# Memory keys before their norm, and a second cross product in the mixer's last row

## The chip, the core and the metric

The kernel runs on one NeuronCore of a Trainium2 chip. The metric is the device time of one execution in microseconds (us). TensorE (PE in the profile) multiplies, VectorE (DVE) and ScalarE (ACT) work element by element, GpSimd (POOL) splits weights, and SyncE (SP) issues nearly all transfers. Each engine runs its own instructions in order; engines meet through semaphores only.

## The reference

One layer on `x` (2048 tokens, width 1024), with a memory of 256 tokens:

```
h = x + W_out [ HGRN2 heads (4) || sliding-window attention heads (8) ](RMSNorm(x, g1))
h = h + CrossAttention_4heads(RMSNorm(h, g2), RMSNorm(mem, gm))
h = h + W_down relu(W_up RMSNorm(h, g3))^2
```

For the cross attention, `kv = RMSNorm(mem, gm) @ wkv`; the first 512 columns are the keys of four heads, each normed again over its 128 entries and scaled by `k_norm_g`; the other 512 are the values. RMSNorm divides a token's vector by the root of its mean square and multiplies by a gain for each of the 1024 entries.

## The kernel before

Matrices lie transposed, 128 rows to a partition tile, tokens along the free dimension. A product of the layer is made from two parts of each operand, a high part rounded to a shorter format and the low rest: for each 128-column panel of weights TensorE runs hi x hi and hi x lo, interleaved, and then lo x hi, 24 matmuls of 512 tokens in all. In an order, `m5.0`, `m5.1`, `m5.2` are the two halves of the first sixteen and the last eight.

There are four functions in a row, each with a block for each engine: `prepare` (norms and projects the memory, norms the first block of the input, makes the rope tables), `mixer` (four blocks of 512 tokens, 22 panels each, with the recurrent and window attention woven in), `cross` and `mlp`. Since an engine never waits at their borders but for semaphores, the border is only a place in each engine's own list.

**`prepare`.** SyncE issues all loads at once: `memT`, the constants, the gains `vec`, half of the key weights `wk`, the input block `hT`, the other half, the values' weights `wv`, the mixer's first two panels. ScalarE squares the memory's eight tiles, VectorE adds them, TensorE sums over partitions with a matrix of ones (L664), ScalarE and VectorE make the root (ScalarE gives a guess from Ln and Exp, VectorE one Newton step), and VectorE multiplies memory, gain `gm` and root into `mn` (L612). Then TensorE makes the keys of heads 0 to 2 (16 passes each), the total of the input's squares (L675), the keys of head 3, the values of the first 128 tokens, the totals of the squared keys, and the other values. ScalarE copies each head's keys out of its bank and squares them. For the input, ScalarE squares (L541) and VectorE adds (L619); behind the total come four ScalarE steps and two of VectorE, and then for each of the eight tiles VectorE's application (L642), ScalarE's high part `hi` and VectorE's low part `lo`. ScalarE's list goes on with the high part of the first mixer panel (`whi`, L560), the first values, the keys' root, the rope tables, the other values. VectorE ends with the keys' root and `memk` (L657). SyncE stores the rope tables, `memk` and `memv` to HBM, and only then goes on to the mixer's panels.

**`mixer`.** The order of each engine's steps is written out by hand in `ORDERS`, one string for each engine and block. `m` makes a product in one of two banks, `t` takes it out, `w` splits a panel's high part on ScalarE (GpSimd makes the low part), `u` turns a tile of probabilities (TensorE transposes, ScalarE copies), `p` multiplies by the values, `T`, `D`, `S`, `o` are the recurrent heads' steps, `A` takes the attention out. ScalarE's list ahead of the first block begins "w18 w19 t17 ...", and TensorE's begins with m17 to m21 of the first block. Three steps of the last row belong to the next stage: `X` and `Y` make the high part of the cross stage's panels 0 and 1 on ScalarE, `X` on GpSimd the low part of panel 0, and `M` on TensorE the first cross product.

At the end of the mixer, ScalarE's step `A3` takes out the last attention tile and issues its store and that of the last recurrent tile. SyncE waits for all four stores of the last row, in

```
            turn(NBLK - 1, True, False)
            for s in stored:
                sp.wait_ge(s.sem, s.at(NBLK - 1, 0))
```

and then begins the list of `cross`: it loads `memk` and `memv`, and then panel 3 as soon as both parts of panel 1 are made. Panel 2 is loaded already. Cross product n (m1, m2, ...) uses panel n in its first turn, in bank n % 2.

Of the kernel before, what the change touches and what calls it, by code (L numbers as in the profile page):

```python
# [22 lines left out]
ALU = mybir.AluOpType  # L23
# [3 lines left out]
P = 128  # L27
# [44 lines left out]
def panel_at(role, u):  # L72
# [96 lines left out]
        "X",  # L169
    ),  # L170
}

# [208 lines left out]
def layer(nc, xT, memT, pos, con_d, vec_d, sinks_d, w_mix, w_cross, w_mk, w_mv, w_mlp, outT):  # L381
# [7 lines left out]
    with ExitStack() as ctx:  # L389
        def sb(name, shape, dt=F32):  # L390
# [10 lines left out]
                  cross_hi=ctx.enter_context(nc.semaphore("c_panel_hi_ready")),  # L401
                  mlp_hi=ctx.enter_context(nc.semaphore("m_weight_hi_ready")),
# [32 lines left out]
def prepare(nc, block, sems, sh, memT, pos, con_d, vec_d, sinks_d, w_mk, w_mv, rope_d, mem_d, xT, w_mix):  # L435
# [9 lines left out]
    with ExitStack() as ctx:  # L445
# [17 lines left out]
        rv = sb("p_rv", [P, 5, MEM])  # L463
        rr = sb("p_rr", [P, 5, MEM])
        ru = sb("p_ru", [P, 5, MEM])
        ksq = sb("ksq", [P, HEADS, MEM])
        kraw = sb("kraw", [P, HEADS, MEM])
        key_mean, key_guess, key_root = (t[:, 1:1 + HEADS, :].rearrange("p h t -> p (h t)") for t in (rv, rr, ru))
# [29 lines left out]
        sh["first_ready"] = s_xhi, s_xln, s_act  # L498

        @block.sync  # L500
        def _(sp):
# [11 lines left out]
            sp.wait_ge(s_kn, 1)  # L513
# [6 lines left out]
        def _(act):  # L520
# [10 lines left out]
            act.activation(rv[:, 0, :], bank[0][:, 0:MEM], ACT.Identity, scale=1.0 / D_MODEL, bias=eps[:])  # L531
            act.activation(rr[:, 0, :], bank[0][:, 0:MEM], ACT.Ln, scale=1.0 / D_MODEL, bias=eps[:]).then_inc(s_act, 1)
            act.wait_ge(s_act, 1)
            act.activation(rr[:, 0, :], rr[:, 0, :], ACT.Exp, scale=-0.5).then_inc(s_r0, 1)
# [18 lines left out]
            act.wait_ge(s_mk, HEADS)  # L553
            act.activation(kraw[:, HEADS - 1, :], bank[HEADS][:, 0:MEM], ACT.Copy)
            act.activation(ksq[:, HEADS - 1, :], bank[HEADS][:, 0:MEM], ACT.Square).then_inc(s_kc, 1)
# [6 lines left out]
            act.activation(memv[:, 0, :], bank[5][:, :], ACT.Copy).then_inc(s_vc, 1)  # L562
            for n in range(HEADS // 2):
                act.wait_ge(s_tot, 3 + n)
                act.activation(key_mean[:, n * TB:(n + 1) * TB], bank[1 + n][:], ACT.Identity, scale=1.0 / P, bias=eps[:])
                act.activation(key_guess[:, n * TB:(n + 1) * TB], bank[1 + n][:], ACT.Ln, scale=1.0 / P, bias=eps[:]).then_inc(s_act, 1)
# [8 lines left out]
            act.activation(memv[:, 1, :], bank[6][:, :], ACT.Copy).then_inc(s_vc, 1)  # L575

        @block.vector
        def _(dve):
# [8 lines left out]
            chained(dve.memset(eps[:], EPS))  # L587
            for k in range(1, KT):
# [5 lines left out]
            dve.wait_ge(s_con, 32)  # L594
# [13 lines left out]
            chained(dve.scalar_tensor_tensor(ru[:, 0, :], rr[:, 0, :], -0.5, rr[:, 0, :], ALU.mult, ALU.mult))  # L608
            chained(dve.tensor_tensor(ru[:, 0, :], ru[:, 0, :], rv[:, 0, :], ALU.mult))
            chained(dve.scalar_tensor_tensor(ru[:, 0, :], ru[:, 0, :], 1.5, rr[:, 0, :], ALU.add, ALU.mult))  # L610
# [79 lines left out]
def mixer(nc, block, sems, sh, xT, w_mix, rope_d, y_d, w_cross, lows_d):  # L690
# [17 lines left out]
    with ExitStack() as ctx:  # L708
# [767 lines left out]
        def _(pe):  # L1476
# [43 lines left out]
            def cross_make(blk, part):  # L1520
# [6 lines left out]
                for k in range(KT) if part == 2 else range(part * KT // 2, (part + 1) * KT // 2):  # L1527
# [3 lines left out]
                    if part < 2:  # L1531
                        pe.matmul(PROJ[0][:], w[:, 0, cols], lo[:, k, :], start=False, stop=False)
# [1779 lines left out]
```

## Time and profile before

| | |
|---|---|
| runs | 2503.6, 2501.66, 2501.6 us; median 2501.66 us |
| the profiled execution | 2495.6 us, its span 2493.8 us |
| granted clock of TensorE, mean | 0.998 of 2.4 GHz |
| `prepare` on TensorE | 11.07 to 47.05 us |
| the mixer on TensorE | 47.05 to 816.4 us |

The span goes from the first to the last instruction of the profiled execution; times in the rows are counted from its start.

### The profile page before, as it was taken

The numbers are of one execution on the slowest core, as the hardware profiler recorded it, in microseconds if no ns is written. First come the engines' busy times: TensorE is split into PE (matmuls) and PEld (weight loads), VectorE is DVE, ScalarE is ACT, GpSimd is POOL, SyncE is SP. The second block draws the span as 40 slices with busy tenths as digits, with TensorE's granted clock in tenths as the row PEclk, the third lists the DMA queues.
The fourth block names the chain that finished last, engine by engine and source line by source line (L and its number), as shares of the span: only waits on it lengthen the run. The fifth ranks groups of instructions, "written<-read, shape, count | busy, mean of one in ns | idle before, by whom it ended". The sixth has DMA issues, their size and how long they took to land.

```text
span 2493.8 us, 39390 instructions
## 1 busy us (share of the span) xinstructions
PE 2454.1 (98%) x14110; PEld 2014.8 (81%) x14110; DVE 1735.3 (70%) x3014; ACT 1136.4 (46%) x2164; POOL 880.0 (35%) x1018
## 2 busy tenths in 40 slices
PE   7999999999999999999999999999999999999999
PEld 5878788888887788788878888788888888888887
DVE  6899788788678474766677767876664545565765
ACT  5575566676666456546653223522232232323231
POOL 1433100000000552564337768476673222222222
PEclk9999999999999999999999999999999999999999
DMA  4442643543532531752343343232348653445664
GB/s 188 169 138 94 210 131 114 204 142 115 206 131 94 199 132 46 254 177 85 106 165 119 131 177 111 92 135 102 123 146 292 201 150 114 141 127 150 209 198 137
DMA packets 189187, 371.54 MB, mean 149 GB/s; under 512 B 14273, under 2 KB 80321, under 8 KB 187073
## 3 DMA queue, kind: packets, MB, share of 16 engines
q1 hardware_dynamic: 183840, 359.51, 43.4%
q10 hardware_dynamic: 5152, 9.51, 1.0%
q8 instruction: 114, 1.87, 0.3%
q14 instruction: 81, 0.66, 0.1%
HBM read 286.71 MB, written 79.89 MB: 147 GB/s over the span
## 4 chain that ended last, share of the span: by engine, by line
PE 64%; DVE 2%; issue 1%; DMA 1%; ACT 1%; POOL 0%; DVEq 0%; ACTq 0%; SPq 0%; POOLq 0%
PE bank L3228 8%; PE bank L3226 8%; PE bank L3230 8%; PE bank L3206 7%; PE bank L3203 7%; PE bank L3202 7%; PE bank L2145 4%; PE bank L2140 4%; PE bank L2141 4%; PE bank L2192 1%; PE bank L2171 1%; PE bank L2182 1%; PE bank L2120 1%; PE bank L3181 0%; PE bank L3186 0%
## 5 line engine op out<-in xcount | busy, mean ns | idle before, releaser
L411 POOL TENSOR_TENSOR wlo<-raw,whi 128x256 fp32r<-128x256 f32 x372 | 312.3, 871 | 942.6 <-ACT whi L1113 520.5
L1506 PE MATMUL bank<-hi,whi 128*128 128x512 f32 x704 | 284.5, 404 | 1.8 <-ACT fg L1076 1.8
L3230 PE MATMUL bank<-hi,wlo 128*128 128x512 f32 x896 | 276.0, 389 | 0.0
L3228 PE MATMUL bank<-lo,whi 128*128 128x512 f32 x896 | 276.0, 389 | 0.0
L3226 PE MATMUL bank<-hi,whi 128*128 128x512 f32 x896 | 276.0, 389 | 0.0
L1509 PE MATMUL bank<-lo,whi 128*128 128x512 f32 x704 | 275.6, 392 | 0.2 <-DVE lo L1257 0.2
L3017 DVE TENSOR_TENSOR lo<-h,hi 128x1024 fp32r<-128x1024 f32 x80 | 124.4, 1554 | 172.9 <-ACT hi L2781 172.9
L2712 POOL TENSOR_TENSOR wlo<-h,whi 128x256 fp32r<-128x256 f32 x160 | 126.8, 815 | 300.0 <-ACT whi L2773 300.0
L2140 PE MATMUL bank<-hi,whi 128*128 128x512 f32 x504 | 202.7, 402 | 1.7 <-DVE h L2033 1.3
L2141 PE MATMUL bank<-lo,whi 128*128 128x512 f32 x504 | 196.8, 390 | 0.0
L3226 PEld LDWEIGHTS bank<-hi,whi 128*128 128x128 f32 x896 | 168.3, 188 | 34.8
L3230 PEld LDWEIGHTS bank<-hi,wlo 128*128 128x128 f32 x896 | 168.3, 188 | 34.8
L3228 PEld LDWEIGHTS bank<-lo,whi 128*128 128x128 f32 x896 | 168.3, 188 | 34.8
L2693 POOL TENSOR_TENSOR wlo<-raw,whi 128x256 fp32r<-128x256 f32 x166 | 151.0, 935 | 123.0 <-ACT whi L2722 115.3
L2773 ACT ACTIVATE whi<-h 128x512 fp32r<-128x512 f32 x80 | 50.6, 632 | 286.8 <-PE bank L3230 268.6
L1516 PE MATMUL bank<-hi,wlo 128*128 128x512 f32 x704 | 178.1, 395 | 0.0
L2693 POOL TENSOR_TENSOR m_xlo<-raw,m_xhi 128x256 fp32r<-128x256 f32 x174 | 165.0, 981 | 0.0
L2722 ACT ACTIVATE whi<-raw 128x512 fp32r<-128x512 f32 x87 | 54.5, 629 | 230.5 <-DMA raw<-w_mlp 186.3
L1506 PEld LDWEIGHTS bank<-hi,whi 128*128 128x128 f32 x704 | 132.3, 188 | 32.5 <-issue 2.9
L1509 PEld LDWEIGHTS bank<-lo,whi 128*128 128x128 f32 x704 | 132.5, 188 | 29.0 <-issue 2.2
L1516 PEld LDWEIGHTS bank<-hi,wlo 128*128 128x128 f32 x704 | 130.8, 188 | 28.9 <-issue 2.2
L3202 PE MATMUL bank<-hi,whi 128*128 128x512 f32 x348 | 136.0, 391 | 1.6 <-issue 1.6
(401 smaller groups left out, 5562.1 us busy)
## 6 DMA issues: line engine op xcount, KB each, us to landing
h<-hidden_scratch SPq DMA_DIRECT2D x96, 512.0 KB, 4.2
raw<-w_mix SPq DMA_DIRECT2D x88, 512.0 KB, 4.3
raw<-w_cross SPq DMA_DIRECT2D x64, 512.0 KB, 3.6
raw<-w_mlp SPq DMA_DIRECT2D x64, 512.0 KB, 4.6
wlo<-mixer_lows_scratch SPq DMA_DIRECT2D x60, 512.0 KB, 3.9
hidden_scratch<-hT SPq DMA_DIRECT2D x116, 256.0 KB, 2.1
h<-w_mlp SPq DMA_DIRECT2D x112, 256.0 KB, 3.0
mixer_lows_scratch<-wlo SPq DMA_DIRECT2D x22, 512.0 KB, 2.9
```

Source lines behind the costliest of these rows:

```text
L411: last = pool.tensor_tensor(wlo[:, i, cols], raw[:, i, cols], whi[:, i, cols].bitcast(F32), ALU.subtract)
L1506: pe.matmul(out, w, hi[:, k, :], start=k == 0, stop=False)
L1509: pe.matmul(out, w, lo[:, k, :], start=False, stop=False)
L1516: last = pe.matmul(out, wlo[:, i % 2, k * P:(k + 1) * P], hi[:, k, :], start=False, stop=k == KT - 1)
L2140: pe.matmul(out, w, hi[b][:, k, :], start=k == 0, stop=False)
L2141: pe.matmul(out, w, lo[b][:, k, :], start=False, stop=False)
L2693: last = pool.tensor_tensor(lo_tile[:, cols], source(half, n, w)[:, cols], hi_tile[:, cols].bitcast(F32), ALU.subtract)
L3202: pe.matmul(acc, hi_tile[:, cols], parts(half, m, k)[0], start=k == 0, stop=False)
L3203: pe.matmul(acc, hi_tile[:, cols], parts(half, m, k)[1], start=False, stop=False)
L3226: pe.matmul(down_bank(i)[:], wh[:, cols], xh[:, i % 2, :], start=K == 0, stop=False)
L3228: pe.matmul(down_bank(i)[:], wh[:, cols], xl[:, i % 2, :], start=False, stop=False)
L3230: last = pe.matmul(down_bank(i)[:], wl[:, cols], xh[:, i % 2, :], start=False, stop=K == KD - 1)
```

## The change

Three things change. In `prepare`, the memory is projected with its gain alone (`mn` is memory times `gm`); the token roots, one number for each of the 256 tokens, are multiplied into the keys by VectorE as it takes them out of their banks, and into the values as a scale by ScalarE. For the values the roots are needed along partitions; two one-column matmuls beside the total give them there, in columns 256 and 257 of the same tiles. The memory's total stands behind head 0 on TensorE, the input's total behind head 3 instead of head 2. The keys use other banks (2, 3, 4, 1), and the mixer no longer waits for the keys' totals but for the four key products. In `mixer`, the last row makes the second cross product too: `M1` in three parts, two of them ahead of `p3`, and `Y` stands directly behind `X`. GpSimd's low part of panel 0 goes from the mixer's list into that of `cross`, behind its count increments.

```diff
-        "o3.0 o3.1 o3.2 o3.3 u12 u13 L3 u14 M0 M1 M2 u15 p3",
+        "o3.0 o3.1 o3.2 o3.3 u12 u13 L3 u14 M0.0 M0.1 M0.2 u15 M1.0 M1.1 p3 M1.2",
...
-        "b3 c8 Q2 w16 t14 u8 L2 c9 c10 c11 t15 e3 t16 l0 l1 l2 n4 l3 u9 X u10 u11 T3 G3 l4 l5 l6 A2 l7 c12 c13 c14 "
-        "u12 Q3 u13 c15 L3 u14 u15 Y A3",
+        "b3 c8 Q2 w16 t14 u8 L2 c9 c10 c11 t15 e3 t16 l0 l1 l2 n4 l3 u9 X Y u10 u11 T3 G3 l4 l5 l6 A2 l7 c12 c13 c14 "
+        "u12 Q3 u13 c15 L3 u14 u15 A3",
...
-        "X",
+        "",
...
+        KEY_BANKS = [bank[n][:, 0:MEM] for n in (2, 3, 4, 1)]
+        KEY_TOTALS = bank[2], bank[3]
...
-            sp.wait_ge(s_kn, 1)
+            sp.wait_ge(s_kn, HEADS + 1)
             sp.dma_start(mem_d[:, 0, :], memk[:].rearrange("p h t -> p (h t)")).then_inc(s_st, 16)
...
-            act.activation(rr[:, 0, :], rr[:, 0, :], ACT.Exp, scale=-0.5).then_inc(s_r0, 1)
+            act.activation(token_guess[:], token_guess[:], ACT.Exp, scale=-0.5).then_inc(s_r0, 1)
...
-            for h in range(3):
-                act.wait_ge(s_mk, h + 1)
-                act.activation(kraw[:, h, :], bank[1 + h][:, 0:MEM], ACT.Copy)
-                act.activation(ksq[:, h, :], bank[1 + h][:, 0:MEM], ACT.Square).then_inc(s_kc, 1)
...
+            for h in range(HEADS):
+                act.wait_ge(s_kn, h + 1)
+                act.activation(ksq[:, h, :], kraw[:, h, :], ACT.Square).then_inc(s_kc, 1)
             for k in range(KT):
                 act.wait_ge(s_mn, KT + k + 1)
                 act.activation(hi[:, k, :], hT[:, k, :], ACT.Copy).then_inc(s_xhi, 1)
...
+            act.wait_ge(s_kn, HEADS)
+            act.activation(memv[:, 0, :], bank[5][:, :], ACT.Identity, scale=token_root[:, MEM + 0:MEM + 1]).then_inc(s_vc, 1)
...
             chained(dve.memset(eps[:], EPS))
+            dve.wait_ge(s_con, 32)
+            dve.wait_ge(s_mem, 16)
+            for k in range(KT):
+                dve.tensor_scalar(mn[:, k, :], mT[:, k, :], v("gm", k, k + 1), None, ALU.mult).then_inc(s_mn, 1)
...
-            for k in range(KT):
-                dve.scalar_tensor_tensor(mn[:, k, :], mT[:, k, :], v("gm", k, k + 1), ru[:, 0, :],
-                                         ALU.mult, ALU.mult).then_inc(s_mn, 1)
             dve.wait_ge(s_msq, KT + 1)
             dve.tensor_copy(nsum[:], sq[:, 0, :]).then_inc(s_sum, 1)
...
+            def key(h):
+
+                dve.wait_ge(s_mk, h + 1)
+                dve.tensor_tensor(kraw[:, h, :], KEY_BANKS[h], token_root[:, 0:MEM], ALU.mult).then_inc(s_kn, 1)
+
+            key(0)
+            key(1)
             dve.wait_ge(s_pos, 16 * (RF + 1))
...
+            key(2)
             dve.wait_ge(s_xln, 4)
...
+                if k == 0:
+                    key(3)
...
-            pe.wait_ge(s_sum, 1)
-            pe.matmul(bank[0][:, 0:MEM], ones, msq[:, 0, :], start=True, stop=True).then_inc(s_tot, 1)
...
-                if h == 2:
+                if h == 0:
+                    pe.wait_ge(s_sum, 1)
+                    pe.matmul(bank[0][:, 0:MEM], ones, msq[:, 0, :], start=True, stop=True)
+                    for n in range(MEM // P):
+                        last = pe.matmul(bank[0][:, MEM + n:MEM + n + 1], msq[:, 0, n * P:(n + 1) * P], ones[:, 0:1],
+                                         start=True, stop=True)
+                    last.then_inc(s_tot, 1)
+                if h == HEADS - 1:
                     pe.wait_ge(s_sum, 1 + KT)
                     pe.matmul(bank[7][:], ones, nsum[:], start=True, stop=True).then_inc(s_tot, 1)
...
                     elif kind == "cross_second":
                         act.wait_ge(set_up, COUNTS_SET)
                         act.wait_ge(*sh["loaded_for_cross"])
+                        act.wait_ge(product.sem, product.at(blk, AHEAD - 2))
...
-            def cross_make(blk, part):
+            def cross_make(blk, n, part):
...
+                if n == 1:
+                    pe.wait_ge((sh["cross_hi"], sh["cross_lo"])[part // 2], CROSS_PAN + 2)
...
-            pe.wait_ge(s_act, 1 + HEADS // 2)
+            pe.wait_ge(s_keys, HEADS)
...
             pool.sem_inc(sh["set_up"], 1)
+            hi_ready, count, lo_ready = sh["first_cross_panel"]
+            pool.wait_ge(hi_ready, count)
+            split_low(pool, 0).then_inc(lo_ready, 1)
```

## Rows read from the trace of the kernel before

**Rows 1.** The page's busy time, share of the span and instructions of each engine.
```profile
PE 2454.1 (98%) x14110; PEld 2014.8 (81%) x14110; DVE 1735.3 (70%) x3014; ACT 1136.4 (46%) x2164; POOL 880.0 (35%) x1018
```

**Rows 2.** Timeline, TensorE, start: start us, us, line, tiles, count [idle before <-releaser].
```profile
15.76 12.09 PE L670 MATMUL bank<-h,wk 128*128 128x256 f32 x48 [3.50 <-DVE h L612]
27.68 1.02 PE L675 MATMUL bank<-p_nsum,con 128*128 128x512 f32 x2
...
60.39 0.50 PE L1506 MATMUL bank<-hi,whi 128*128 128x512 f32 x1 [1.84 <-ACT fg L1076]
```

**Rows 3.** Timeline, TensorE, the mixer's end and the first cross products.
```profile
789.52 0.66 PE L1658 MATMUL bank<-con,s_sb 128*128 128x128 f32 x4 [0.69 <-ACT pT L1198]
...
814.45 1.97 PE L1668 MATMUL bank<-pT,vsw 128*64 128x128 f32 x32 [0.73 <-ACT pT L1198]
...
820.11 1.98 PE L2145 MATMUL bank<-hi,wlo 128*128 128x512 f32 x8
...
828.39 0.47 PE L2140 MATMUL bank<-hi,whi 128*128 128x512 f32 x1 [0.86 <-DVE h L2033]
```

**Rows 4.** Timeline, ScalarE, start.
```profile
12.36 0.47 ACT L531 ACTIVATE p_rv<-bank,eps 128x256 f32<-128x256 f32 x1 [2.90 <-PE bank L664]
...
16.71 3.47 ACT L541 ACTIVATE p_sq<-hT 128x512 f32<-128x512 f32 x6 [2.97 <-DMA hT<-xT]
...
28.74 0.69 ACT L547 ACTIVATE p_nmean<-bank,eps 128x512 f32<-128x512 f32 x1 [0.20 <-PE bank L675]
...
42.52 1.04 ACT L560 ACTIVATE whi<-raw 128x1024 fp32r<-128x1024 f32 x1
...
58.80 1.06 ACT L1109 ACTIVATE whi<-raw 128x1024 fp32r<-128x1024 f32 x1 [6.46 <-DMA raw<-w_mix]
```

**Rows 5.** Timeline, SyncE, start: the issue of transfers.
```profile
2.11 0.65 SPq L505 DMA_DIRECT2D wk<-w_mk  x1
...
52.58 0.33 SPq L514 DMA_DIRECT2D memory_scratch<-memk  x1
...
53.67 2.00 SPq L926 DMA_DIRECT2D raw<-w_mix  x2
```

**Rows 6.** Timeline, ScalarE, the mixer's end and the start of cross.
```profile
788.87 0.60 ACT L1198 ACTIVATE pT<-bank 128x512 f32<-128x512 f32 x1
...
814.25 1.05 ACT L1117 ACTIVATE whi<-raw 128x1024 fp32r<-128x1024 f32 x1
...
827.19 1.06 ACT L1937 ACTIVATE whi<-raw 128x1024 fp32r<-128x1024 f32 x1 [8.53 <-DMA raw<-w_cross]
```

**Rows 7.** Transfers issued in the first 3 us: queue, count, KB, us to landing.
```profile
wk<-w_mk SPq DMA_DIRECT2D x1, 1024.0 KB, 8.9
...
vec<-vec_d SPq DMA_DIRECT2D x1, 22.5 KB, 7.4
```

**Rows 8.** Timeline, VectorE, start.
```profile
7.74 2.72 DVE L591 TENSOR_TENSOR h<-h 128x256 f32<-128x256 f32 x6 [6.88 <-ACT h L528]
...
15.13 3.26 DVE L612 SCALAR_TENSOR_TENSOR h<-h,vec,p_ru 128x256 f32<-128x256 f32 x8
...
18.83 5.47 DVE L619 TENSOR_TENSOR p_nsum<-p_nsum,p_sq 128x512 f32<-128x512 f32 x7
...
31.36 0.69 DVE L638 TENSOR_TENSOR p_nsum<-p_nsum,p_nmean 128x512 f32<-128x512 f32 x1 [3.66 <-ACT p_nsum L552]
```

**Rows 9.** TensorE in two stretches: us, busy (matmul passes begun), granted clock, DMA share, GB/s.
```profile
17.00:18.00 1.00, 1.00 (x3) 1.00 0.98 418
...
22.00:23.00 1.00, 1.00 (x7) 1.00 0.92 393
```

**Rows 10.** Timeline, SyncE, the start of cross.
```profile
819.65 0.33 SPq L1821 DMA_DIRECT2D c_memk<-memory_scratch  x1
...
820.61 1.13 SPq L1867 DMA_DIRECT2D raw<-w_cross  x1
```

**Rows 11.** Transfers of cross panels issued between 760 and 850 us, with their median.
```profile
raw<-w_cross SPq DMA_DIRECT2D x10, 512.0 KB, 4.6
```

More of the change, by code:

```diff
@@ L462, in prepare @@
         wv = sb("wv", [P, KT, HEADS * P])
-        rv = sb("p_rv", [P, 5, MEM])
-        rr = sb("p_rr", [P, 5, MEM])
-        ru = sb("p_ru", [P, 5, MEM])
+        rv = sb("p_rv", [P, HEADS, MEM])
+        rr = sb("p_rr", [P, HEADS, MEM])
+        ru = sb("p_ru", [P, HEADS, MEM])
+        both = MEM + MEM // P
+        token_mean, token_guess, token_root = (sb(f"p_token_{n}", [P, both]) for n in ("mean", "guess", "root"))
         ksq = sb("ksq", [P, HEADS, MEM])
         kraw = sb("kraw", [P, HEADS, MEM])
-        key_mean, key_guess, key_root = (t[:, 1:1 + HEADS, :].rearrange("p h t -> p (h t)") for t in (rv, rr, ru))
+        key_mean, key_guess, key_root = (t[:].rearrange("p h t -> p (h t)") for t in (rv, rr, ru))
         lbt = sb("lbt", [P, 8, HEADS])
@@ L530, in _ @@
             act.wait_ge(s_tot, 1)
-            act.activation(rv[:, 0, :], bank[0][:, 0:MEM], ACT.Identity, scale=1.0 / D_MODEL, bias=eps[:])
-            act.activation(rr[:, 0, :], bank[0][:, 0:MEM], ACT.Ln, scale=1.0 / D_MODEL, bias=eps[:]).then_inc(s_act, 1)
+            act.activation(token_mean[:], bank[0][:, 0:both], ACT.Identity, scale=1.0 / D_MODEL, bias=eps[:])
+            act.activation(token_guess[:], bank[0][:, 0:both], ACT.Ln, scale=1.0 / D_MODEL, bias=eps[:]).then_inc(s_act, 1)
             act.wait_ge(s_act, 1)
-            act.activation(rr[:, 0, :], rr[:, 0, :], ACT.Exp, scale=-0.5).then_inc(s_r0, 1)
+            act.activation(token_guess[:], token_guess[:], ACT.Exp, scale=-0.5).then_inc(s_r0, 1)
             act.wait_ge(s_dve, BOUND_MAX)
@@ L574, in _ @@
             act.wait_ge(s_mk, HEADS + 2)
-            act.activation(memv[:, 1, :], bank[6][:, :], ACT.Copy).then_inc(s_vc, 1)
+            act.activation(memv[:, 1, :], bank[6][:, :], ACT.Identity, scale=token_root[:, MEM + 1:MEM + 2]).then_inc(s_vc, 1)
         @block.vector
@@ L684, in _ @@
                     for h in range(HEADS):
-                        last = pe.matmul(bank[1 + h // 2][:, h % 2 * MEM:(h % 2 + 1) * MEM], ones, ksq[:, h, :], start=True, stop=True)
+                        last = pe.matmul(KEY_TOTALS[h // 2][:, h % 2 * MEM:(h % 2 + 1) * MEM], ones, ksq[:, h, :], start=True, stop=True)
                         if h % 2:
@@ L1528, in cross_make @@
                     cols = slice(k * P, (k + 1) * P)
-                    last = pe.matmul(PROJ[0][:], w[:, 0, cols], hi[:, k, :], start=(part, k) == (0, 0),
+                    last = pe.matmul(PROJ[n][:], w[:, n, cols], hi[:, k, :], start=(part, k) == (0, 0),
                                      stop=(part, k) == (2, KT - 1))
                     if part < 2:
-                        pe.matmul(PROJ[0][:], w[:, 0, cols], lo[:, k, :], start=False, stop=False)
+                        pe.matmul(PROJ[n][:], w[:, n, cols], lo[:, k, :], start=False, stop=False)
                 if part == 2:
@@ L1742, in cross @@
         signals.append(w_hi)
-        w_lo = signal("c_panel_lo_ready", CROSS_PAN)
+        w_lo = Signal(sh["cross_lo"], CROSS_PAN, 1)
+        signals.append(w_lo)
         signals.append(Signal(sh["cross_product"], len(CROSS_PRODUCTS)))
@@ L2153, in _ @@
                 if kind == "make":
-                    if (turn, step[1]) != (0, 0):
+                    if (turn, step[1]) not in ((0, 0), (0, 1)):
                         make(turn, step[1], step[2])
```

34 lines of the change are left out of this document (14 added, 20 removed).

## The prediction, made before the change was timed

> **What bounds the kernel now.** First the page's busy shares: TensorE is busy for 2454.1 us, 98% of the span [rows 1], so only 39.7 us of 2493.8 are open to an edit that leaves TensorE its work. Then TensorE's timeline, for the idle time in brackets: 14.6 us of it stand before the memory projection begins at 15.76, and one of 1.84 us before the third mixer product of the first row, at 60.39 [rows 2]; the edits touch these and the tail of the mixer [rows 3]. Behind both the products follow one another, so what moves the product behind a gap moves the end by about as much. Third, who ends each gap: not the engine the change is about. At 60.39 it is `t17`, which ScalarE runs behind `w19`, and `w19` began at 58.80 after 6.46 us of waiting for a panel [rows 4]. SyncE issued that panel at 53.67, straight after the store of `memk` at 52.58 [rows 5]. In the tail, the product m3 at 828.39 is charged to VectorE's `h`, but ScalarE's split of its panel ran from 827.19 to 828.25 and had waited 8.53 us for the load [rows 3, 6]; that is the late one.
>
> **The start: earlier keys.** The root leaves the path to the keys. Eight gain multiplies now need only `mT` and `vec`; `vec` is issued just ahead of `wk` and lands 7.4 us on, by 9.5 [rows 5, 7]. I price them as the old applications, 3.26 / 8 = 0.41 each [rows 8]: done by 12.8. `wk`'s first half lands at 2.11 + 8.9 = 11.0 [rows 5, 7], so keys begin near 11.05, 4.7 us earlier. Head 0 won't be quick: before, three passes came per us at 17 to 18 and seven at 22 to 23 [rows 9]; 48 passes took 27.68 - 15.76 = 11.9 us [rows 2], and with two heads at 3.45 (16 passes at the later pace) the first took 5.0 us. So key 0 ends near 16.1. The sum of squares, seven adds at 0.45 behind the multiplies [rows 8], is ready at 16.0: no wait there. Its total, 1.0 us with the four one-column passes, ends at 17.1 and now stands on TensorE's path.
>
> Then the input's own norm is squeezed. The token root's ScalarE steps start at 17.3 instead of 12.36 and take 1.3 us, and only behind them can ScalarE square the input: at 18.65 instead of 16.71 [rows 4]. VectorE, 1.4 us for the new root, starts summing at 20.0 and ends at 26.0, 1.7 us later than 24.30 [rows 8]. That is still ahead of TensorE, which finishes key 3 at 17.1 + 3 x 3.45 = 27.5; the input's total behind it begins at 27.5, before at 27.68 [rows 2]. So ScalarE starts the input's root at 28.55 instead of 28.74 [rows 4]. Of the 4.7 us 0.2 are left: 3.45 went into head four, 1.0 into the memory's total.
>
> VectorE has two key products (0.45 each, as an add of this shape [rows 8]) and the 3.4 us of angles between 26.0 and 30.4, then key 2 until 30.85; the root is ready at 31.15 (before 31.36 [rows 8]). Key 3 stands behind the first application of the root: 0.45 us on VectorE, and one more square on ScalarE before the first `hi`, some 0.2 us more that VectorE waits for. The last `hi`, and with it the panel split `whi`, at 42.52 before [rows 4], comes at 42.52 - 0.2 + 0.6 = 42.9. From there ScalarE's queue is the same and had no idle time: the key root, then `memk`, its store and the panel all come 0.4 us later, and m19 too. The removed TensorE wait on the key totals lets m17 begin near 44.5, 2.5 us sooner, and buys nothing: TensorE stands longer before m18 and m19. The four `kraw` copies leave ScalarE where it was waiting for TensorE, and the values' copies only get a scale: I cost both at nothing, and with that cover gone it would be some 0.3 us a copy. **Start: +0.4 us**; from -0.3 (a pace of 0.31 on VectorE and no wait for key 3) to +1.5 (the sums late by a us, so that they set the input's total).
>
> **The tail: two moves against each other.** (a) `Y` goes from behind `u15`, where ScalarE waited for TensorE anyway, to behind `X`. There the copy of `u10` starts at 788.87, and TensorE's turn at 789.52 has waited 0.69 us for it [rows 3, 6]. One whole panel copy is 1.05 us [rows 6]; TensorE ended `u10` only at 788.83, so some 0.1 of it is covered: `u10` and all that hangs on it in series (`u11`, `T3`, `D3`, the state, the last scores) come 0.9 us later. The second low split on GpSimd runs there beside VectorE; VectorE waits for TensorE before the state, so I cost it at nothing; the whole share that it could take there is below the 0.9 that the state is late anyway. `X` on GpSimd goes behind its count increments, where GpSimd idles: nothing. (b) M1.0 and M1.1 go between `u15` and `p3`. The 16 matmuls take 820.11 - 816.42 = 3.7 us and cover the 0.73 us that `p3` waited [rows 3]. TensorE saves 0.73, and `p3` itself ends 3.7 - 0.73 + 0.9 = 3.9 us later, at 820.3 instead of 816.42.
>
> What is queued behind `p3`: ScalarE's `A3`, its two stores, and then SyncE, which waits for every store of the mixed tiles before it issues `memk`, `memv` and panel 3. Before, that began at 819.65, and panel 3 stood at the queue's head from 820.61, in a row of 1.13 us [rows 10] where such an issue takes 0.33 [rows 5]: 0.8 us of it is the wait for the low split of panel 1, which is now long done. Now SyncE goes on 3.9 us later, at 823.5, and issues panel 3 at 824.5. Its landing was 7.5 us behind the first of these issues; without the 0.8 it is 6.7, at 830.3, and m3, 1.2 us behind it as before, begins at 831.5 instead of 828.39: **+3.1 us**. TensorE, through with M1.2 at 822.1 and with m2 at 827.5, then stands for up to 3.9 us (before 0.86). Below: a panel's median landing, 4.6 us [rows 11], from 824.5 gives 829.1 and m3 at 830.3, +1.9; with (a) absorbed as well, +1.0. Above: the whole shift of 3.9. I take 3.1, since its row has the same three transfers.
>
> The row shows three transfers of 512 KB issued within 2 us and the last landing 7.5 us behind the first [rows 6, 10]. The Trainium skill, "DMA: Bandwidth & Descriptors", section "Queues, rings and completion order", says that descriptors of one queue are consumed in ring order; by that the panel waits out `memk` and `memv`, and the sum is nearer +3.9 than the median's +1.9. No run here shows the two apart yet.
>
> **Sum.** 0.4 + 3.1 = +3.5 us. The profiled execution took 2495.6 us with its span of 2493.8; the median of the runs is 2501.66, 6.1 above, and I add the shift to the median: **2505.2 us**. The three runs differ by 2.0 us, and what a measurement here tells from no change is 0.2%, 5.0 us. So I forecast no change that can be told, on the later side.
>
> **Rivals.**
> 1. *The longer stalls cost pace too (slower).* Behind the 3.5 us gap at 15.76 the first head took 5.0 us instead of 3.45, 1.55 us more [rows 2, 9]; behind the 1.84 us gap at 60.39 the first matmul took 0.50 and nothing followed. If the new stalls, up to 3.9 us before m3 and 2.6 before m19, act like the first, the sum is 3.5 + 2 x 1.55 = 6.6: 2508.3. It decides from 1.5 us on, which one of them just gives. Against it: the profile's granted clock reads 1.00 in all of this [rows 9], the full 2.4 GHz, and TensorE has worked without a break for long before either stall, as it had not before 15.76. The Trainium skill, "TensorE: Matmul & The Clock Gate", Part 1, says that the lower clock is the default, that activity lifts it and an idle stretch brings it back; by that rule the pace after each new stall would be halved at first. The trace bears it out only by the pace at 17 us, not by its clock column. Chance 0.17.
> 2. *Panel 3 isn't the gate.* If its load was issued early enough and m3 waited for VectorE, as the row has it, the tail gives -0.73 - 0.86 + 0.9 = -0.7 and the whole -0.3: 2501.4. Against it: `w3` ended 0.1 us before m3 and had waited for its load. Chance 0.14.
> 3. *The earlier mixer start stays.* If m19 followed m18 without a gap, 2.5 us would be gained, and the sum is -2.5 + 3.1 = +0.6: 2502.3. Against it: the panel for m19 hangs on `memk`, not on TensorE. Chance 0.05.
> 4. *Faster by more than 5 us*: the trace has no gap that the change could close and that is that long; the start gap less than 4.7 us and the tail's 1.6 would both have to be kept whole. Chance 0.03.
>
> My forecast has 0.61. Of it, the upper bounds together (+1.5 and +3.9) reach 5.4, just over the 0.2%: a chance of 0.03 of it counts as slower. So slower 0.20, the same 0.77, faster 0.03. The range goes from 2501.0 (below rivals 2 and 3, at the lower bounds, +0.7, less part of the runs' spread) to 2508.3 (rival 1).
>
> **What would show it.** After: keys begin near 11 and the input's total behind head 3 at 27.5; `whi` of m17 at 42.9; m17 near 44.5, a gap of over 2 us before m18 and one before m19, which starts at 60.8. In the tail `p3` without a wait, ending 3.9 us later; the `memk` load issued near 823.9 (0.4 from the start comes on top of all these times); m3 behind a gap of 3 to 4 us, charged to a load or ScalarE's split. Wrong if m19 starts before 60, if panel 3 is issued before 822, or if `u10`'s copy isn't late.

## The result, and the profile after the change

| | before | after |
|---|---|---|
| median (20 runs each, on the same chip) | 2498.38 us | 2505.07 us |
| lowest and highest run | 2494.71, 2503.6 us | 2499.76, 2508.95 us |
| ratio, 95% interval | | 1.0023, 1.0016 to 1.003 |
| the profiled execution, its span | 2495.6, 2493.8 us | 2508.95, 2507.1 us |

The change makes the kernel slower by 0.23%, 5.7 us by the ratio (6.7 us by the medians). The interval does not contain 1, and lies on both sides of the 0.2% that the prediction takes for what can be told. That the measured 2505.07 us is so near the predicted 2505.2 is luck: the forecast was a shift of +3.5 us on a median of 2501.66, over more runs that median is 2498.4, and a base 3.3 us too high made up for a shift that was 2 to 3 us too small.

The two profiled executions overstate the difference: the one after is the slowest of its 20 runs, and the one before lies under its median. Behind m3 all programs of this study have the same work, and from the start of m3 to the end of the span they take between 1664.5 us (gates_off, below) and 1669.5 us (after). So I read positions up to m3 from profiles, and what a version costs from the medians. Against before, m3's shift and the ratio of the runs agree within 1.5 us in twelve of the thirteen versions below. The change itself is the exception: in its profile m3 stands 9.2 us later where the runs say 5.7, so what is added up along that profile is more than the change costs on average.

The page after; the first line answers to [rows 1]. TensorE works 4.4 us longer, at the same count of passes but for four, which is a first hint of the clock.

```profile
PE 2458.5 (98%) x14114; PEld 2016.6 (80%) x14114; DVE 1735.5 (69%) x3018; ACT 1136.5 (45%) x2160; POOL 884.1 (35%) x1018
```

TensorE's timeline after, at the start: start us, duration, line, tiles, count, and in brackets the idle time before and who ended it. It answers to [rows 2].

```profile
11.23 5.28 PE L679 MATMUL bank<-h,wk 128*128 128x256 f32 x16 [11.23 <-DMA wk<-w_mk]
...
17.14 10.61 PE L679 MATMUL bank<-h,wk 128*128 128x256 f32 x48
27.59 1.02 PE L691 MATMUL bank<-p_nsum,con 128*128 128x512 f32 x2
...
44.36 0.47 PE L1520 MATMUL bank<-hi,whi 128*128 128x512 f32 x1 [0.29 <-ACT whi L560]
...
53.21 0.47 PE L1520 MATMUL bank<-hi,whi 128*128 128x512 f32 x1 [3.13 <-ACT whi L1122]
...
61.05 0.50 PE L1520 MATMUL bank<-hi,whi 128*128 128x512 f32 x1 [2.12 <-ACT fg L1089]
...
62.36 0.63 PE L1523 MATMUL bank<-lo,whi 128*128 128x512 f32 x1
62.79 0.63 PE L1520 MATMUL bank<-hi,whi 128*128 128x512 f32 x1
```

Keys begin 4.5 us earlier and the input's total is where it was. m17 starts 2.7 us earlier, and the time comes back as two waits: 3.13 us before m18, which did not wait before, and 2.12 us before m19, which waited 1.84. Then something new: about a us after m19 has begun, its passes come 0.43 us apart (62.36, 62.79) instead of the 0.23 at its beginning. Who holds m19 is in ScalarE's timeline after, whose rows answer to [rows 4, 6]: still a load.

```profile
43.07 1.04 ACT L560 ACTIVATE whi<-raw 128x1024 fp32r<-128x1024 f32 x1
...
59.46 1.06 ACT L1122 ACTIVATE whi<-raw 128x1024 fp32r<-128x1024 f32 x1 [6.39 <-DMA raw<-w_mix]
...
836.40 1.06 ACT L1958 ACTIVATE whi<-raw 128x1024 fp32r<-128x1024 f32 x1 [9.15 <-DMA raw<-w_cross]
```

And in SyncE's timeline after, against [rows 5, 10], that load (L943) still stands behind the memory's two stores:

```profile
53.22 0.33 SPq L518 DMA_DIRECT2D memory_scratch<-memk  x1
53.59 0.43 SPq L520 DMA_DIRECT2D memory_scratch<-memv  x1
54.31 12.90 SPq L943 DMA_DIRECT2D raw<-w_mix  x4
...
828.26 0.33 SPq L1839 DMA_DIRECT2D c_memk<-memory_scratch  x1
828.64 1.30 SPq L1840 DMA_DIRECT2D c_memv<-memory_scratch  x1
830.10 0.33 SPq L1885 DMA_DIRECT2D raw<-w_cross  x1
```

TensorE after, at the mixer's end, against [rows 3].

```profile
792.65 0.66 PE L1675 MATMUL bank<-con,s_sb 128*128 128x128 f32 x4 [1.52 <-ACT pT L1212]
...
802.15 1.35 PE L1663 MATMUL bank<-ksw,qk 64*128 64x256 f32 x8 [2.48 <-DVE state L1388]
804.68 2.08 PE L1663 MATMUL bank<-ksw,qk 64*128 64x256 f32 x8 [1.18 <-DVE stat L1463]
...
823.02 1.97 PE L1685 MATMUL bank<-pT,vsw 128*64 128x128 f32 x32
...
837.61 0.76 PE L2161 MATMUL bank<-hi,whi 128*128 128x512 f32 x1 [4.51 <-ACT whi L1958]
```

p3 has lost its wait and starts 8.6 us later than in [rows 3]; m3 starts 9.2 us later, with a wait of 4.51 us instead of 0.86. Its releaser is now ScalarE's split at 836.40, which had waited 9.15 us for the load that SyncE issued at 830.10.

Last, TensorE in four stretches of the profile before: us, busy (in brackets the passes that fall in the stretch, wholly or in part), granted clock, DMA share, GB/s. This is the view that I had read only at 17 and 22 us [rows 9]; there too the count is not of passes begun, which are two at 17 to 18 us and five at 22 to 23.

```profile
62.00:65.40 3.40, 3.40 (x17) 1.00 0.45 145
802.40:809.60 7.20, 6.36 (x85) 1.00 0.16 43
828.40:832.00 3.60, 3.60 (x16) 1.00 0.54 170
837.60:841.00 3.40, 3.40 (x17) 1.00 0.67 222
```

And the same four stretches after:

```profile
62.00:65.40 3.40, 3.40 (x11) 0.54 0.25 76
802.40:809.60 7.20, 6.02 (x70) 0.54 0.27 107
828.40:832.00 3.60, 3.60 (x17) 1.00 0.62 191
837.60:841.00 3.40, 3.39 (x9) 0.58 0.68 202
```

Behind three of the longer waits (those of m19, the last scores and m3) TensorE ran for some us at the lower of its two clocks, 1.2 GHz: 11 passes fall in 3.4 us instead of 17. Behind m18's 3.13 us it did not; its passes stay 0.23 us apart. A busy share of 100% hides a lower clock; only the count of passes and the clock show it.

These four stretches are picked from the profile after. The kernel before runs at the lower clock elsewhere, in this same tail too, behind waits of 0.69, 0.69 and 1.53 us. TensorE before:

```profile
793.90:797.20 3.30, 3.30 (x34) 0.53 0.02 5
```

At least a part of that is hidden, since the scores behind it still waited 0.56 us for VectorE's state. So in the tail the change moved the lower clock from here to the scores, where it lasts about twice as long (802.9 to 809.7 us); only the stretches behind m19 and m3 are new.

Added up along the profile after, for u15, which starts at 818.81 instead of 813.12, so 5.69 us later: m19 late 0.66; the slower passes behind it 1.63 (at 787 us all stands 2.29 us later); Y before u10's copy 0.84 (u11 then stands 3.13 later); VectorE's later state (some 0.3), and the scores and what follows at half clock (some 2.2), the remaining 2.56. From u15 to p3 M1's two parts add 3.6 and take away the wait of 0.7: 8.57.

### The profile page after: what moved, and what is told of

It reads as the page before. It is cut to its first block, busy times and chain, and to the rows that moved or that the text cites. A ratio compares the mean times of both kernels' runs of the same rounds, so it can differ in the third digit from the quotient of the medians.

```text
span 2507.1 us, 39399 instructions
## 1 busy us (share of the span) xinstructions
PE 2458.5 (98%) x14114; PEld 2016.6 (80%) x14114; DVE 1735.5 (69%) x3018; ACT 1136.5 (45%) x2160; POOL 884.1 (35%) x1018
## 4 chain that ended last, share of the span: by engine, by line
PE 60%; DVE 2%; issue 2%; POOL 2%; DMA 1%; ACT 1%; SPq 0%; DVEq 0%; ACTq 0%; POOLq 0%
PE bank L3247 8%; PE bank L3249 8%; PE bank L3251 8%; PE bank L3227 6%; PE bank L3223 6%; PE bank L3224 6%; PE bank L2166 4%; PE bank L2161 4%; PE bank L2162 4%; PE bank L2213 1%; PE bank L2192 1%; POOL m_xlo L2714 1%; POOL wlo L2714 1%; DMA raw<-w_mlp 1%; PE bank L2203 1%
```

## The experiments

Medians vary by a us or two between sets of runs, so the ratio to runs of the kernel before on the same chip is the measure. Positions are from one profile each; "split 3" is ScalarE's high part of panel 3.

| version | median us | ratio, 95% interval | m19 | p3 | split 3 | m3 |
|---|---|---|---|---|---|---|
| before | | 1 | 60.39 | 814.45 | 827.19 | 828.39 |
| after | 2505.07 | 1.0023 (1.0016 to 1.003) | 61.05 | 823.02 | 836.40 | 837.61 |
| start_only | 2499.37 | 1.0006 (0.9998 to 1.0015) | 61.02 | 816.49 | 830.15 | 831.35 |
| tail_only | 2503.66 | 1.0025 (1.0015 to 1.0035) | 60.78 | 821.15 | 834.56 | 835.76 |
| p3_first | 2499.38 | 1.0012 (1.0002 to 1.0023) | 62.12 | 816.78 | 829.58 | 830.79 |
| panel3_early | 2500.12 | 1.0009 (1.0 to 1.0017) | 61.81 | 819.54 | 822.71 | 829.46 |
| m1_half | 2503.49 | 1.0023 (1.0014 to 1.0032) | 61.81 | 819.60 | 833.10 | 834.30 |
| warm | 2507.81 | 1.0041 (1.0029 to 1.0054) | 63.90 | 822.97 | 834.77 | 839.37 |
| warm_fit | 2501.35 | 1.0014 (1.0005 to 1.0023) | 60.76 | 820.29 | 832.17 | 833.37 |
| warm_start | 2497.52 | 0.9997 (0.9988 to 1.0005) | 61.79 | 815.05 | 827.71 | 828.91 |
| total_head2 | 2497.01 | 0.9996 (0.9987 to 1.0005) | 61.11 | 812.90 | 827.00 | 828.20 |
| start_loads | 2499.86 | 1.0006 (0.9998 to 1.0015) | 59.21 | 813.85 | 827.36 | 828.56 |
| gates_off | 2493.11 | 0.9981 (0.9972 to 0.9989) | 57.57 | 811.06 | 818.81 | 823.99 |
| gates_off_old_start | 2494.52 | 0.9989 (0.998 to 0.9998) | 59.10 | 813.37 | 821.10 | 826.28 |

### Which half costs: start_only, tail_only

start_only keeps the change's `prepare` and puts the tail's two moves back (M1 stays in the mixer, behind p3):

```diff
-        "... u14 M0.0 M0.1 M0.2 u15 M1.0 M1.1 p3 M1.2"
+        "... u14 M0.0 M0.1 M0.2 u15 p3 M1.0 M1.1 M1.2"
-        "... l3 u9 X Y u10 ... u14 u15 A3"
+        "... l3 u9 X u10 ... u14 u15 Y A3"
```

tail_only keeps the change's orders and takes `prepare` from the kernel before, with the mixer's wait on the keys' totals.

start_only:

> The change's start, with the tail in the old order (Y behind u15, p3 ahead of M1). Theory A (the loss is made of a later panel and a lower clock behind each new stall): m19 begins at 61.0 as with the whole change (60.4 before), and where the granted clock falls there, 1.5 us more: +0.7 to +2.3 us against before. Rival B (the start's shift alone makes the loss): the whole loss of the change, +5.7. Rival C (the earlier mixer start stays): faster by some 2.

tail_only:

> The old start with the change's tail (Y behind X, M1.0 and M1.1 ahead of p3). Theory A: the larger part, +4 to +7 us: p3 ends some 5 later, panel 3 is issued as much later, and TensorE stalls 4 to 5 us before m3, with the clock at half behind it for 3 us. Rival B: nothing, within 1 us of before.

Nearly all of the cost is in the tail: +0.25% alone, against +0.06% for the start, which by itself can't be told from nothing. The two don't add up exactly (0.31% against 0.23%), within the intervals.

### What in the tail costs: p3_first, panel3_early, m1_half

p3_first is the whole change with p3 in front of all of M1; Y stays behind X. m1_half is the dose between: M1.0 alone ahead of p3. panel3_early keeps the change's orders and has SyncE issue panel 3 in the mixer's last row, ahead of the waits for the stores, on a semaphore of its own:

```diff
                 if last:
                     sp.wait_ge(set_up, COUNTS_SET)
+                    for ready in (sh["cross_hi"], sh["cross_lo"]):
+                        sp.wait_ge(ready, CROSS_PAN + 2)
+                    sp.dma_start(raw[:, 1, :], w_cross[CROSS_SOURCE[3]]).then_inc(sh["cross_raw_in_1"], 16)
                     wait_all(sp, sh["split_for_cross"])
```

p3_first:

> The whole change, but p3 stands ahead of all of M1, and Y stays behind X. Theory A: panel 3 is no longer late against TensorE, so the stall before m3 falls from 4.5 us to 1 or less and the clock stays up there: 4 to 5 us less than the whole change, about +1 to +3 against before. Rival D (Y on ScalarE and the second low split beside VectorE make the tail's loss): no more than 1 us less than the whole change.

panel3_early:

> The whole change, and SyncE issues the load of panel 3 in the mixer's last row, as soon as both parts of panel 1 are made, ahead of the last stores and of memk and memv. Theory A (the load behind p3's stores is the gate): no stall of over 1 us before m3, m3 straight behind m2, 5 to 6 us less than the whole change and near before, -1 to +2. Rival D: a stall before m3 stays, since m2 and m3 are late by ScalarE and VectorE, and it is within 1 us of the whole change.

m1_half:

> The whole change with only a half of the high part of panel 1's product (M1.0, 8 passes, 1.85 us) between u15 and p3, where the change puts M1.0 and M1.1. A dose between the change (2505.1 us) and p3 in front of all of M1 (2499.4 us). Theory A (panel 3's load waits behind p3's outputs, and product 3 behind that load): p3 comes 1.8 us earlier than in the change, product 3 waits about 2.7 us instead of 4.5, and the time is 1.8 to 3.5 us under the change, 2501.5 to 2503.3 us. Rival: u15's copy of 0.7 us is all that matters there, M1.0 hides it, and the time is at or under 2499.4 us. Second rival: product 3 is held by the panels' loads at a fixed place; then the wait stays at 4.5 us and the time at 2505 us.

panel3_early is the clean cut. p3 is as late as in m1_half (819.5), but the load no longer hangs on it. SyncE's timeline of panel3_early has the issue of panel 3 at 801.73, between a store and panel 2's load; ScalarE then splits panels 2 and 3 in one go, and m3 follows m2 without a bracket.

```profile
801.73 0.37 SPq L997 DMA_DIRECT2D raw<-w_cross  x1
809.65 0.33 SPq L999 DMA_DIRECT2D raw<-w_cross  x1
```

ScalarE's timeline of panel3_early:

```profile
822.71 2.01 ACT L1962 ACTIVATE whi<-raw 128x1024 fp32r<-128x1024 f32 x2 [0.53 <-ACT h L1222]
```

TensorE's timeline of panel3_early, the end of m2 and the start of m3:

```profile
827.65 1.98 PE L2170 MATMUL bank<-hi,wlo 128*128 128x512 f32 x8
829.46 0.39 PE L2165 MATMUL bank<-hi,whi 128*128 128x512 f32 x1
```

So a late p3 costs little of its own (panel3_early stands at +0.09%, start_only at +0.06%); what costs is the load behind its stores. The table says the same the other way round: in the versions that leave panel 3 where it was, p3 starts anywhere from 812.90 to 823.02 us, and split 3 follows it by 11.8 to 14.1 us each time. Rival 2 of the prediction (panel 3 isn't the gate) falls.

m1_half went half as expected. In its profile m3 waits 3.42 us and stands 3.3 us ahead of the change's, as a dose between should; its median does not show that (1.0023, as the change), and lies 0.2 us above what was expected. With intervals of 0.09% to either side I can't tell 1.8 us of dose from none.

### What the lower clock costs: warm, warm_fit, warm_start

Plain matmuls of the constants, 128x512, into a bank that is free, stand on TensorE just ahead of the waits, so that it works while it would stand.

```diff
                 if part == 0:
+                    if blk == -1 and i in (AHEAD + 1, AHEAD + 2):
+                        for _ in range(3 if i == AHEAD + 1 else 2):
+                            pe.matmul(bank[7][:], c("ones"), con[:, 0:TB], start=True, stop=True)
                     pe.wait_ge(copied.sem, copied.at(blk, i - 2))
```

warm and warm_fit are the whole change with these and the like before the last head's scores and before m3; warm_start is start_only with those before m18 and m19 alone.

warm:

> The whole change, with plain matmuls of the constants (128x512, about 0.48 us each, into a free bank) put on TensorE in front of four of its waits: 6 before panel 18's product, 4 before panel 19's, 4 before the last head's scores, 8 before the cross stage's product 3. They fill 2.9, 1.9, 1.9 and 3.8 us of waits that the profile after puts at 3.13, 2.12, 2.48 and 4.51 us; the output is the same. Theory A (waits, and on top of them the granted clock that falls after each): the products start where they did, within 0.3 us, the granted clock at 62-65, 802-810 and 837-841 us goes from 0.50-0.58 back to 1.00, and the passes at 0.43 us apart go back to 0.23: 1.6 us back at the start, up to 3 at 802-810, 1.5 after product 3, so 3 to 5 us under the change, 2500 to 2502 us. Rival: the slower clock costs nothing that another engine's wait does not take anyway; then the clock is back and the time stays at 2505 us. Second rival: the clock falls somewhere else instead; then the drops are as many and the time stays too.

warm_fit:

> warm again with fewer matmuls: in warm each took 0.88 us and not 0.48, so they filled 5.3, 3.6, 3.7 and 7.0 us where the waits were 3.1, 2.1, 2.5 and 4.5, and were late themselves. Now 3, 2, 2 and 4 of them fill 2.6, 1.8, 1.8 and 3.5 us. Theory A (waits, and on top of them the granted clock that falls behind each): the products start within 0.3 us of where they stood in the change, no stretch at 61-68, 802-812 and 836-843 us is under 0.97, and 3 to 5 us come back: 2500 to 2502 us. Rival: the slower clock costs nothing of its own: 2505 us.

warm_start:

> start_only (2499.4 us; clock down at 61-68 us in its profile) with 3 such matmuls before panel 18's product and 2 before panel 19's. Theory A: the drop at 61-68 us is gone, panel 20's product starts 1.6 us earlier, and the time is 1 to 2 us under start_only, 2497.4 to 2498.4 us, that of total_head2 (2497.0 us), whose wait before panel 18 was only 0.66 us and whose clock stayed up there. Rival: 2499.4 us, and total_head2 was faster for another reason.

warm missed its aim: I had priced a matmul at 0.48 us and it took 0.88, so the fillers were late themselves, and with the clock up the kernel was slower than the change. TensorE's timeline of warm_fit, where they fit:

```profile
49.85 2.73 PE L1515 MATMUL bank<-con 128*128 128x512 f32 x6
53.15 0.47 PE L1523 MATMUL bank<-hi,whi 128*128 128x512 f32 x1 [0.57 <-ACT whi L1122]
...
58.70 1.88 PE L1515 MATMUL bank<-con 128*128 128x512 f32 x4
60.76 0.50 PE L1523 MATMUL bank<-hi,whi 128*128 128x512 f32 x1 [0.19 <-ACT fg L1089]
```

m18 and m19 start where they started in the change, within 0.3 us: nothing was gained on the waits. But in the same four stretches of warm_fit the clock is up:

```profile
62.00:65.40 3.40, 3.40 (x16) 1.00 0.32 110
802.40:809.60 7.20, 5.12 (x85) 1.00 0.12 44
828.40:832.00 3.60, 3.60 (x14) 1.00 1.02 402
837.60:841.00 3.40, 3.40 (x17) 1.00 0.88 254
```

It is not up everywhere. Ahead of the fillers before the last scores, where the change has 1.00, warm_fit runs at half clock for 6.8 us:

```profile
792.60:799.40 6.80, 5.38 (x47) 0.50 0.00 0
```

So behind m19 and m3 the lower clock is gone, and in the tail it has only moved, by some 10 us, which the second rival of warm's expectation had expected of every stretch.

And time came back: 2501.35 against 2505.07 us, 3.7 us by the medians and 0.09%, 2.2 us, by the ratios, whose intervals overlap. warm_start repeats it for the start: 0.9997 against start_only's 1.0006, again 0.09% with overlapping intervals. Not all of that need be the clock's: split 3 follows p3 by 11.88 us in warm_fit and by 13.38 in the change, by 12.66 in warm_start and by 13.66 in start_only, and that split waits for its load, not for a filler.

A third reading needs no fillers. The mean granted clock of each run is on record, for the kernel before in 93 runs of the three sets that most of the ratios rest on: nine runs at 1.000 took 2494.2 us on average, 25 at 0.997 took 2500.6, some 2.1 us for each 0.001. The change's runs have 0.996 on average and those of before 0.998, which gives an estimate of some 4 us, if the clock makes the time and does not only go along with it. Three readings point the same way, and none shows it alone: I take the lower clock to have cost 2 to 4 us of the change's time.

### What the start could give: total_head2, start_loads

total_head2 is start_only with the input's total behind head 2, as before the change (`if h == HEADS // 2:`). start_loads is start_only with two steps moved: SyncE loads panel 19 ahead of the three stores, as soon as panel 17's low part is made, and ScalarE makes panel 18's high part ahead of the sines:

```diff
+            sp.wait_ge(sh["w_lo"], AHEAD + 1)
+            sp.dma_start(raw[:, AHEAD % 2, :], w_mix[AHEAD + 2]).then_inc(sh["raw_in_1"], 16)
             sp.wait_ge(s_sin, 3)
...
             act.activation(key_guess, key_guess, ACT.Exp, scale=-0.5).then_inc(s_r0, 1)
+            act.activation(sh["whi"][:, 1 - AHEAD % 2, :], sh["raw"][:, 1 - AHEAD % 2, :], ACT.Copy).then_inc(sh["w_hi"], 1)
```

total_head2:

> The change's start with the old order of the tail, as in start_only (2499.4 us), but the input's total behind head three of the key projection instead of behind head four. Theory A: ScalarE's root of the input follows VectorE's sum (26.2 us) instead of the last keys (27.6 us), so panel 17's product starts about 1.1 us earlier, at 43.3 us, and so does all that follows, panel 19's product at 59.9 us; about 1 us under start_only, 2498.3 us. Rival: the last head's keys, their product with the roots and their squares come later instead and hold the norm's first products on VectorE and so the high parts; then panel 17's product stays at 44.4 us and the time at 2499.4 us.

start_loads:

> The change's start with the old order of the tail, as in start_only (2499.4 us), and two steps moved: SyncE loads panel 19 as soon as panel 17's low part is done (about 47 us), ahead of the stores of the angles and of the memory, instead of behind them (54.3 us); and ScalarE makes panel 18's high part behind the key roots (48 us), ahead of the sines, instead of behind the second memory value (52 us). Theory A (the products that the change's start sets free run into these two waits): panel 18's product starts at about 49.9 us without its 3.1 us wait, panel 19's at 56 to 57.5 us instead of 61.0, the drop of the clock at 61-68 us is gone, and the lead of 3.5 to 5 us stays to the end: 2494.5 to 2496 us, under the kernel before. Rival C: the loads and splits of row 0's panels set its pace, the lead is gone by row 1, and the time is 2498 to 2499.5 us.

total_head2 was faster than expected and for another reason than expected. The input's total began at 27.03, only 0.4 us earlier than in start_only, and TensorE stood 1.93 us for VectorE's sum; m18 and m19 start within 0.1 us of where they do in the change. But m17 runs later, so the long wait before m18 is gone. TensorE's timeline of total_head2:

```profile
27.03 1.12 PE L691 MATMUL bank<-p_nsum,con 128*128 128x512 f32 x2 [1.93 <-DVE p_nsum L620]
...
53.21 0.47 PE L1520 MATMUL bank<-hi,whi 128*128 128x512 f32 x1 [0.66 <-ACT whi L1122]
...
61.11 0.50 PE L1520 MATMUL bank<-hi,whi 128*128 128x512 f32 x1 [2.20 <-ACT fg L1089]
```

And its clock behind m19, in the stretch that read 0.54 in the change:

```profile
62.00:65.40 3.40, 3.40 (x17) 1.00 0.21 66
```

The same wait of some 2.2 us before m19 was followed by the lower clock where m18 had waited 3.1 us (start_only), and by the full clock where m18 had waited 0.66 (total_head2). TensorE's work is the same in both; putting the input's total behind head 3 only pulled m17 away from m18. In panel3_early, p3_first and m1_half the drop came behind m18's wait already, at 53 to 60 us; the wait before m19 then shrank to 0.84 us at most, and m19 stood later, at 61.8 to 62.1. These three have the change's start unaltered, so which of the two waits the lower clock follows is not settled by the program. total_head2 is not free of it either: its clock falls behind m3's wait of 2.22 us, at 829 us.

In start_loads m18 did not wait for its panel's high part, but 1.28 us for GpSimd's low part in its middle, and m19 came only 1.8 us earlier. The next gate took over: ScalarE's t17, which writes where `prepare` kept its tiles, waits until the memory's stores have landed (ScalarE, start_loads):

```profile
58.56 0.60 ACT L1097 ACTIVATE fg<-bank 128x512 f32<-128x512 f32 x1 [4.73 <-DMA memory_scratch<-memv]
```

The median shows none of those 1.8 us (1.0006, as start_only). Rival C of that run's expectation has the time nearly right, but not the way to it: the lead is not gone by row 1, p3 stands 2.6 us and m3 2.8 us ahead of start_only's in the profiles. Where it goes behind m3 stays open.

### All gates at once: gates_off, gates_off_old_start

gates_off is the change with the input's total behind head 2, the early load of panel 19, Y behind u15, panel 3's load issued in the mixer's last row (behind the residual's load), and the low part of panel 0's product between u15 and p3, where it covers the copy that p3 waits for:

```diff
-        "... u14 M0.0 M0.1 M0.2 u15 M1.0 M1.1 p3 M1.2"
+        "... u14 M0.0 M0.1 u15 M0.2 p3 M1.0 M1.1 M1.2"
```

gates_off_old_start has all of that but the input's total, and the `prepare` of the kernel before.

gates_off:

> The change with its gates moved: the input's total behind head three; panel 19 loaded as soon as panel 17's low part is done; Y behind u15; the order u14 M0.0 M0.1 u15 M0.2 p3 M1.0 M1.1 M1.2, in which the low part of panel 0's product hides u15's copy; and SyncE loads cross panel 3 in the mixer's last row, as soon as panel 1 is split, ahead of the waits for the stored outputs. Theory A: panel 19's product starts near 59 us instead of 61.1, p3 has no wait of 0.7 us, product 3 none of 2.2 us; 2 to 5 us under total_head2 (2497.0 us): 2492 to 2495 us, under the kernel before. Rival C: what comes early is given back to the next wait, 2497 us.

gates_off_old_start:

> gates_off with the preparation of the kernel before (norm ahead of the projection) and all its moved loads and orders. It tells whether the change's start is worth anything once its gates are open. Theory A: panel 17's and 18's products are held by ScalarE's chain and the memory's stores in both, so the two are within 1 us of each other, 2493 to 2496 us. Rival: the start that projects first is worth its 2 to 3 us as soon as nothing holds the panels; then this one is 2 to 3 us over gates_off.

gates_off is under the kernel before by 0.19% (0.11 to 0.28%). p3 and m3 have no wait (u15 now waits 1.13 us for u14's copy), m3 starts at 823.99, and the mean granted clock of its profile is 1.00. With the old start the gain is 0.11% (0.02 to 0.20%). What each of the five moves brings was not measured apart. What the new start adds in this company is 1.4 us by the medians, between the two expectations and inside the intervals, and m19 1.5 us earlier in the profiles; whether it is worth anything there stays undecided.

## Why the prediction was right, and where it was not

**The start, +0.4: right in place and size.** Keys at 11.23 (I said 11.05), the input's total at 27.59 (27.5), panel 17's split at 43.07 (42.9), m17 at 44.36 (44.5), m19 at 61.05 (60.8). It came 0.66 us later than in [rows 2], since the store of memk and the panel behind it came 0.64 later [rows 5]. The gain multiplies took 2.19 us for eight, 0.27 each where I had 0.41; that bought nothing, since keys wait for `wk`.

**"Buys nothing: TensorE stands longer before m18 and m19": wrong.** It bought a loss. The second of the two waits, 3.13 and 2.12 us, is followed by the lower clock, and that cost 1.63 us in the profile after. In the medians the start by itself can't be told from nothing (start_only, +0.06%).

**Y behind X, +0.9: right.** u11's wait went from 0.69 to 1.52 us, +0.83. The second low split "costed at nothing" was not quite: GpSimd's two splits run without a break at 791.24 to 798.75, and VectorE runs beside them. VectorE's timeline after, ahead of the state:

```profile
797.21 0.94 DVE L1369 TENSOR_SCALAR eg<-eg 128x512 f32<-128x512 f32 x1
798.08 0.75 DVE L1382 COPY st<-state 128x128 f32<-128x128 f32 x1
798.98 2.65 DVE L1388 SCALAR_TENSOR_TENSOR st<-st,span,bank 128x128 f32<-128x128 f32 x7
```

The same three before, where GpSimd's one split had ended at 792.6:

```profile
794.47 0.42 DVE L1355 TENSOR_SCALAR eg<-eg 128x512 f32<-128x512 f32 x1
794.80 0.22 DVE L1368 COPY st<-state 128x128 f32<-128x128 f32 x1
795.52 2.65 DVE L1374 SCALAR_TENSOR_TENSOR st<-st,span,bank 128x128 f32<-128x128 f32 x7 [0.50 <-PE bank L1572]
```

Two operations are 1.05 us longer together, and the cover that I named, VectorE's wait of 0.50 us for TensorE before the state, is gone. (That wait stood behind a product of TensorE's that fell in the lower clock before, 2.00 us at 793.48, and takes 1.16 after.) The state (its first row, 798.98 against 795.52) comes 3.46 us later, where u11 comes 3.13 later: some 0.3 us got through. Y's place alone hardly matters to the median (p3_first against start_only, 0.06% apart, inside the intervals).

**Two parts of M1 ahead of p3, panel 3 late, +3.1: the mechanism is shown, the size was low.** The working had p3 3.0 us later than u15's shift, and it came 2.9 later. It had the load land 6.7 us behind SyncE's first issue, since the 0.8 us in [rows 10] that I took for a wait on panel 1's low part would fall away; they did not, the same time stands in c_memv's row of 1.30 us, and the split began 8.1 us behind. In warm, warm_fit and warm_start that row is 0.42 to 0.43 us, and the split began 6.6 to 6.7 us behind, as in the working; what takes the time in the others no run told. The three loads land in the order of their issue (after: memk 4.2 us from its issue, at 832.5, memv 6.3, at 834.9, the panel by 836.4, at most 6.3 from its own), where a panel's median is 4.6 [rows 11]. That fits a panel that waits out the two ahead of it, but a shared rate would look alike. The upper bound of +3.9 for the tail was nearer than the +3.1 that I took; tail_only has +0.25%, 6.2 us, with the clock in it.

**Rival 1, the pace behind the stalls, was the missing term.** The forecast's terms put u15 1.3 us later (0.4 and 0.9), and it came 5.69 later; of the 4.4 us between, 1.63 are the slower passes behind m19 and some 2.2 those at the last scores. For the stall before m19 the rival's price, 1.55 us, was nearly right. I gave it 0.17, and against it that the granted clock read 1.00 and that TensorE had worked long before either stall. Neither says what comes behind a stall, and the column is no proof either: it reads 1.00 at 17 to 18 us [rows 9], where the passes began 0.43 us apart, and 0.22 later in the same product. The Trainium skill, "TensorE: Matmul & The Clock Gate", Part 1, names the lower clock as the default to which an idle stretch leads back. The trace agrees behind m19 and m3: 0.54 and 0.58 behind waits of 2.12 and 4.51 us, and 1.00 there when fillers took their place. Not every such wait is followed by it, as m18's in the change and m19's in total_head2 show, and before had it behind waits of 1.53 us at most.

**Rivals 2 and 3 fell**: panel 3 is the gate, and the mixer's earlier start is lost. Of the numbers, the shift was +5.7 instead of +3.5. warm_fit's +0.14% is 3.5 us, the forecast's sum, but its interval reaches from 0.05 to 0.23% and it still has lower clock in the tail, so that the two meet is no proof of the terms. Whether the change can be told from none is a matter of tenths: the interval, 0.16 to 0.30%, lies on both sides of the 0.2%.

## What to carry to other kernels

When work leaves one place and the product behind it is held by something else, the gain doesn't vanish, it becomes a wait, and a wait on TensorE can be followed by some us at half clock: price it, and count passes per us over the whole profile, since the busy share hides it and a stretch picked beforehand can miss where it went. When a step is put behind other work, follow every store and every load that its queue issues behind it; here a fill of 3.6 us saved 0.73 us of wait and held a panel's load back by the other 2.9. Moving that load ahead of the wait took the change from +0.23 to +0.09% (panel3_early); with more moves of the kind (gates_off) the time came under that of the kernel before.

## What the runs showed of the hardware

- TensorE's lower clock can come with the first pass or after it: the first passes of m19 after ran 0.23 us apart and only from 62.36 on 0.43, while m3's second pass came 0.56 us behind its first and the next ones 0.43.
- The clock's column does not show all of it: at the first products after, from 11.2 to 14.3 us, passes began 0.43 us apart, then 0.22, and the column reads 1.00 throughout (11 to 16 us).
- A 128x512 matmul of plain 32-bit constants took 0.88 us, as two passes of 0.44 (in warm, twelve passes in a row of 5.31 us); passes of the rounded parts follow each other at 0.23.
- VectorE's 128x512 multiply by a scalar took 0.94 us beside GpSimd's subtraction and 0.42 alone, a 128x128 copy 0.75 and 0.22.
